# An encoder of mixers and feed-forward layers on one core: the even mixer with the k projection folded into q, gate rows in column groups, and another order of its loop

## The reference

```python
def even_mixer(x, w_in, w_out, ...):
    u_m, z_m, u_r, g_r = _split(x @ w_in, EVEN_SIZES)
    y_m = mlstm_mixer(u_m, z_m, ...)
    y_r = rglru_mixer(u_r, g_r, ...)
    return jnp.concatenate([y_m, y_r], axis=-1) @ w_out

def mlstm_mixer(u, z, ...):
    c = jax.nn.silu(dw_conv(u, conv_w, conv_b))
    q = blockdiag(c, wq)                       # blocks of 4 x 4
    k = blockdiag(c, wk) / math.sqrt(ML_DH)
    v = blockdiag(u, wv)
    i_pre = einsum(qkv, w_ig) + b_ig           # two directions, four heads
    log_f = log_sigmoid(einsum(qkv, w_fg) + b_fg)
    ...
    return jax.nn.sigmoid(z) * head_norm(h_f + h_b, norm_g, ML_HEADS, True)

def rglru_direction(x, w_a, b_a, w_x, b_x, lam):
    r = jax.nn.sigmoid(blocks(x, w_a) + b_a)
    i = jax.nn.sigmoid(blocks(x, w_x) + b_x)
    a = jnp.exp(-LRU_C * r * jax.nn.softplus(-lam))
    b = jnp.sqrt(1 - a * a) * i * x
    return linear_recurrence(a, b)             # a scan over 256 positions
```

## Time and profile before

| | |
|---|---|
| median of 3 runs | 2524.05 us (2523.3 to 2526.69) |
| span of the profiled execution | 2525.1 us, one core |
| TensorE busy | 2462.0 us, 98% |
| VectorE, ScalarE, GpSimd busy | 1339.9, 902.7, 1054.3 us |
| read from HBM | 216.02 MB |
| even stage | about 394 to 793 us of the span |

### The profile page before, as it was taken

One profiled execution on the slowest core, in us unless ns is written; L12 is line 12 of the kernel. 1 busy time (PEld: TensorE's weight loads), 2 busy tenths in 40 slices (PEclk: granted clock), 3 DMA queues, 4 the chain that ended last, 5 costly groups with the idle time before them and its releaser, 6 DMA issues.

```text
span 2525.1 us, 35148 instructions
## 1 busy us (share of the span) xinstructions
PE 2462.0 (98%) x13062; PEld 2014.1 (80%) x13062; DVE 1339.9 (53%) x1547; ACT 902.7 (36%) x1171; POOL 1054.3 (42%) x484
## 2 busy tenths in 40 slices
PE   8999999998998999999999999999999999999998
PEld 7888886776777888888888888777777887888887
DVE  3333447997777333245333245687887457433335
ACT  3222226786344222214222214455544333322212
POOL 5444443332225444445444445333333334444443
PEclk9999999998999999999999999999999999999999
DMA  5233322221112332322232332222222222233322
GB/s 167 92 100 98 103 79 69 73 63 45 61 53 79 96 99 96 109 92 75 96 100 92 108 110 75 82 79 76 76 77 75 67 84 81 78 99 97 107 92 79
DMA packets 63780, 219.55 MB, mean 87 GB/s; under 512 B 10920, under 2 KB 15016, under 8 KB 63552
## 3 DMA queue, kind: packets, MB, share of 16 engines
q1 hardware_dynamic: 63120, 216.03, 26.5%
q0 software_dynamic: 560, 2.11, 0.2%
HBM read 216.02 MB, written 2.10 MB: 86 GB/s over the span
## 4 chain that ended last, share of the span: by engine, by line
PE 84%; DVE 8%; ACT 4%; issue 2%; POOL 1%; DMA 0%; ACTq 0%; DVEq 0%; POOLq 0%; SPq 0%
PE ps L506 24%; PE ps L508 24%; PE ps L507 24%; PE ps L537 2%; DVE sb_th L1803 1%; PE ps L962 1%; DVE sb_Up L1961 1%; PE ps L663 1%; PE ps L662 1%; PE ps L488 1%; PE ps L661 1%; PE ps L489 1%; PE ps L494 1%; PE ps L667 1%; DVE sb_x L1699 1%
## 5 line engine op out<-in xcount | busy, mean ns | idle before, releaser
L415 POOL TENSOR_TENSOR sb_wl<-sb_raw,sb_wh 128x1024 fp32r<-128x1024 f32 (+1 forms) x376 | 980.9, 2609 | 1399.7 <-ACT sb_wh L1136 1399.6
L1136 ACT ACTIVATE sb_wh<-sb_raw 128x1024 fp32r<-128x1024 f32 (+1 forms) x376 | 419.1, 1115 | 1287.4 <-PE ps L508 1220.7
L506 PE MATMUL ps<-sb_xh,sb_wh 128*128 128x512 f32 x2096 | 831.1, 397 | 1.0 <-DVE sb_rq L2047 0.5
L508 PE MATMUL ps<-sb_xl,sb_wh 128*128 128x512 f32 x2096 | 816.5, 390 | 0.0
L507 PE MATMUL ps<-sb_xh,sb_wl 128*128 128x512 f32 x2096 | 816.1, 389 | 0.0
L506 PEld LDWEIGHTS ps<-sb_xh,sb_wh 128*128 128x128 f32 x2096 | 393.4, 188 | 87.8 <-issue 5.3
L507 PEld LDWEIGHTS ps<-sb_xh,sb_wl 128*128 128x128 f32 x2096 | 393.7, 188 | 82.3 <-issue 3.1
L508 PEld LDWEIGHTS ps<-sb_xl,sb_wh 128*128 128x128 f32 x2096 | 393.4, 188 | 82.4
L1611 DVE SCALAR_TENSOR_TENSOR sb_hf<-sb_sg,ps 128x512 f32<-128x512 f32 x88 | 60.5, 688 | 590.5 <-PE ps L508 565.3
L506 PE MATMUL ps<-sb_hh,sb_wh 128*128 128x512 f32 x616 | 239.7, 389 | 0.8 <-POOL sb_wl L415 0.8
L508 PE MATMUL ps<-sb_hl,sb_wh 128*128 128x512 f32 x616 | 239.7, 389 | 0.0
(11 more groups left out here) (336 smaller groups left out, 2912.5 us busy)
## 6 DMA issues: line engine op xcount, KB each, us to landing
sb_raw<-w_in SPq DMA_DIRECT2D x176, 512.0 KB, 3.5
sb_raw<-w_out SPq DMA_DIRECT2D x64, 704.0 KB, 4.0
sb_raw<-w_od SPq DMA_DIRECT2D x80, 512.0 KB, 3.5
sb_raw<-w_ev SPq DMA_DIRECT2D x40, 512.0 KB, 3.5
sb_raw<-w_evo SPq DMA_DIRECT2D x8, 512.0 KB, 3.5
sb_raw<-w_odo SPq DMA_DIRECT2D x8, 512.0 KB, 3.5
sb_x<-x_in SPq DMA_DIRECT2D x8, 256.0 KB, 5.7
out<-sb_x SPq DMA_DIRECT2D x16, 128.0 KB, 1.8
```

The lines of the kernel that those rows point to most:

```text
L415: pool.tensor_tensor(wl[:, sl.par, 0:n], raw[:, sl.par, 0:n], wh[:, sl.par, 0:n].bitcast(F32), ALU.subtract).then_inc(lo_done, 1)
L506: pe.matmul(out, w_h, rh(k), start=start and k == 0, stop=False)
L508: mm = pe.matmul(out, w_h, rl(k), start=False, stop=stop and k == kt - 1)
L1136: act.activation(wh[:, sl.par, 0:kt * P], raw[:, sl.par, 0:kt * P], ACT.Copy).then_inc(hi_done, 1)
```

## The change

- **k is folded into q.** A constant, wkr, holds the blocks of wk; VectorE multiplies it with wq's at the start, and q' = c (wq wk^T) then meets c itself in the scores. The tile k_all holds c, the silu's output, and no k is computed or copied.
- **Gate rows.** The weights sb_gw are 32 columns wide. `inner` adds to four groups of 32 PSUM partitions by 256 columns, one for each part (c or u) and sequence. After the loop two products with a constant, gsel, sort the rows, and all gate arithmetic runs on 100 partitions (ROWS) by 256.
- **Order in the loop.** `inner(t - 1)` stands on TensorE behind slot m of pass t and ahead of `lru_gates(t)`. On VectorE, lru_conv(t + 1) and the weights of pass t + 1 (sb_bd, two of three, double-buffered, and sb_gw) stand behind scans(t) and ahead of recurrent_out(t). On ScalarE the copy to sb_lum and the split of slot u + 2 stand between decay and decay_root, and the copies of q and v ahead of the gate tanhs of the next pass.
- **Heads.** negM and thr are broadcast from four row quadrants, in pairs by sequence (`neg_max`, `margin`); the epsilon is taken out of head_norm (`head_eps`) and stands between the two maxima of the next head; slots z and f are dealt anew (EV_SEQ, EV_GAP1, EV_GAP2), and the product for the values uses other PSUM banks and stands behind the first neg_max of the next head.
- **Constants.** Ten DMAs in place of eight.

```diff
 for t, name in ((vec, "vec"), ..., (gb, "gb"), (sel, "sel"),
+                (wkr, "wkr"), (gsel, "gsel")):
     pool.dma_start(t[:], a[name]).then_inc(const_in, 16)
...
 # TensorE, inner(t)
-pe.matmul(ps[:, bq, :], bd[:, 0, :], cc[:], ...).then_inc(q_mm, 1)
-pe.matmul(ps[:, bk, :], bd[:, 1, :], cc[:], ...).then_inc(k_mm, 1)
-pe.matmul(ps[:, 6, :], gw[:, 0, :], cc[:], start=t == 0, stop=False)
-pe.matmul(ps[:, 6, :], gw[:, 1, :], u, start=False, stop=t == KD - 1)
+pe.wait_ge(lu_ev, min(t + 2, KD))
+pe.matmul(ps[:, Q_BANK, :], bd[:, t % 2, 0, :], k_all[:, t, :], ...).then_inc(q_mm, 1)
+for s_ in range(2):
+    for q in range(SEQS):
+        y = CW * (2 * s_ + q)
+        mm = pe.matmul(ps[y:y + CW, 6, 0:L], gw[:, t % 2, s_, :],
+                       um[:, q, 2:2 + L] if s_ else k_all[:, t, part(q)], ...)
...
 # TensorE, the loop
+for t in range(1, KD):
+    pe.wait_ge(u_ev, t)
+    of_x(0, sl(ev_m(t)))
+    inner(t - 1)
+    lru_gates(t)
+    if t < KD - 1:
+        pe.wait_ge(q_ev, t)
+        of_x(1, sl(ev_u(t + 1)))
+    pe.wait_ge(vt_ev, t)
+    of_x(2, sl(ev_g(t)))
...
 # VectorE, the loop
-if t < KD - 1:
-    lru_conv(t + 1)
 scaled_input(t)
 scans(t)
-if t < KD - 1:
-    recurrent_out(t)
+if 1 <= t < KD - 1:
+    lru_conv(t + 1)
+    weights(t + 1)
+recurrent_out(t)
...
 # VectorE, the heads
     dve.tensor_tensor(rec[:, d, :], rec[:, d, :], ps[:, 4 + d, :], ALU.max).then_inc(dmax_done, 1)
+    if d == 0 and h >= 1:
+        head_eps(h - 1, 7, rs[:])
...
 # order of the sixteen slots of the heads
+EV_SEQ = ("z00", "z01", "f0", "f1", "f2", "f3", "z10", "z11", "f4", "f5", "z20", "z21", "f6", "z30", "z31", "f7")
+EV_GAP1 = ((26,), (29,), (32, 33), (36,))
+EV_GAP2 = ((27, 28), (30, 31), (34, 35), (37, 38))
```

More of the change, by code:

```diff
@@ L799, in early_out, with neg_max @@
[L799 to L808, removed]
+                def neg_max(h, q):
+                    pe.wait_ge(mb_mm, 4 * h + 2 * q)
+                    for d in range(2):
+                        y = CW * (2 * d + q)
+                        pe.matmul(ps[:, 2 + d, part(q)], sel[y:y + NH, h, :], negM[y:y + NH, :], start=True,
+                                  stop=True).then_inc(mb_mm, 1)
@@ new lines, in margin, with values @@
+                def margin(h, q):
+                    pe.wait_ge(marg_mm, 4 * h + 2 * q)
+                    for d in range(2):
+                        y = CW * (2 * d + q)
+                        pe.matmul(ps[:, 4 + d, part(q)], sel[y:y + NH, h, :], thr[y:y + NH, :], start=True,
+                                  stop=True).then_inc(marg_mm, 1)
+                def values(h):
+                    pe.wait_ge(att_done, h + 1)
+                    for z in range(HT):
+                        for q in range(SEQS):
+                            for sb_ in range(SB):
+                                o = (HT * h + z) * P
+                                mm = pe.matmul(ps[:, 4 + z, q * L:(q + 1) * L], vT[:, q * SB + sb_, o:o + P],
+                                               att[:, q, sb_, :], start=sb_ == 0, stop=sb_ == SB - 1)
+                    mm.then_inc(pv_mm, 1)
@@ L829, in even @@
+                        neg_max(h, 0)
+                        values(h - 1)
+                        neg_max(h, 1)
+                        if h >= 2:
+                            pe.wait_ge(hvar_in, h - 1)
+                        keys_queries(h)
+                    for n in EV_GAP1[h]:
+                        head_slot(n)
+                    if h == 0:
                         pe.wait_ge(thr_done, 1)
                         pe.wait_ge(gT_ev, 1)
-                        for d in range(2):
-                            margin(d)
@@ new lines, in even @@
+                split(KD, sl(4))
+                silu(0)
+                lru_in(1)
+                split(KD, sl(5))
+                gelu(0)
+                gates(0)
+                decay(0)
+                decay_root(0)
+                for t in range(1, KD):
+                    last = t == KD - 1
+                    split(KD, sl(ev_m(t) + 2))
+                    query_out(t - 1)
+                    inner_in(t)
+                    value_out(t - 1)
+                    gates(t)
+                    silu(t)
+                    decay(t)
+                    if not last:
+                        lru_in(t + 1)
@@ L1332, in even @@
                         split(KD, sl(ev_u(t + 1) + 2))
[L1333 removed]
                     decay_root(t)
[L1335 to L1341 removed]
+                    split(KD, sl(ev_g(t) + 2))
+                    gelu(t)
                 ln_and_exp()
+                act.wait_ge(rows_mm, 1)
@@ L1381, in even @@
                         act.activation(E[:], E[:], ACT.Exp).then_inc(e_done, 1)
-                    if h >= 1:
-                        act.wait_ge(att_done, h)
+                    for n in EV_GAP1[h]:
+                        split(KD, sl(n + 2))
                     for d in range(2):
```

462 lines of the change are left out of this document (208 added, 254 removed).

## The result

| | before | with the change |
|---|---|---|
| median | 2525.37 us (4 runs, 2523.3 to 2526.87) | 2556.87 us (4 runs, 2555.78 to 2559.12) |
| ratio | | 1.0127, 95% interval 1.0115 to 1.0139 |
| span of the profiled execution | 2525.1 us | 2554.0 us |

The change makes the kernel 31.5 us slower. One execution each of two later experiments (e9 and e11) was disturbed and is left out of their ratios; the trace of e11 is of that one, and no row of it is read.

The account below looks back on a forecast made before the run. It took a closed loop over ScalarE and VectorE (12.7 + 11.9 = 24.6 us a pass) as the bound, not TensorE. Its terms, +20.4 + 2.4 - 0.6 - 5.1 + 3.1 + 3.6 - 3.5 + 1.1, sum to +21.4: 2545 us, range 2528 to 2558.

Parts of the forecast that it names:

- The closed loop: Passes 1 to 6, ScalarE and VectorE: lru_conv and weights enter the loop, period 24.6 to 28.0 us, +20.4 in all.
- the rival of a third meeting: A third GpSimd subtraction slips behind the root and delays VectorE: 12.6 us more, 2558; chance 0.08.
- Lower clock of TensorE: Gates after TensorE's wait for sb_lx run at 1.2 GHz, delaying the fourth tanh by some 0.4: +2.4 over six passes.
- Passes 0 and 1: -0.6: Gates of pass 0 behind one slot and the gelu, +1.6; a 2.2 stretch in pass 1 goes; together -0.6 us.
- From the last gates to the first head: -5.1: Gate arithmetic on 100 partitions by 256: first early output slot ends at 40.0 us where it was 45.1.
- Heads: +3.1 and +3.6: Fourteen pairs at 0.63 us replace three visits of 1.91: +3.1; head_eps holds up att_done, 1.2 in heads 1 to 3: +3.6.
- Tail: -3.5: Hole of 3.2 ahead of the last head_var and 2.1 of lower clock go; 1.1 and 0.7 come back.
- Column groups: TensorE's gate rows, four products of 32 columns by 256: 0.63 us instead of 1.72, 1.1 us saved a pass.
- Start: +1.1: Two more DMAs on GpSimd's queue, 0.53 us each, ahead of a subtraction TensorE already waits for: +1.1 us.
- The rival that TensorE is the bound: TensorE's 98% busy sets the time, so its savings and the closed holes count: about 2499 us; chance 0.05.
- the loop without any meeting: Rival: both subtractions fall into ScalarE's part, pass 23.8 us, six passes give -4.8: about 2516; chance 0.08.

Follow-up runs that it names:

- e9: e6 plus a GpSimd wait for mix_done(t - 1) before the subtraction for slot g(t) in passes 1 to 6: 2517.1 us, ratio 0.996.
- e11: The kernel before with only the GpSimd wait for mix_done before the subtraction for slot g(t): 2522.7 us, ratio 0.9991.
- e8: The changed kernel with four more, useless products on TensorE ahead of lru_gates in each of passes 2 to 7: 2552.8 us.
- e1: The changed kernel with lru_conv(t + 1) and the weights put back ahead of scaled_input(t) on VectorE: 2542.8 us, ratio 1.0067.
- e6: The changed kernel with the edits of e1 and e2, and the copy to sb_lum and split of slot u + 2 ahead of decay: 2518.8 us.
- e2: The changed kernel with ScalarE's split of slot 5 moved behind decay(0): 2551.0 us.
- e5: The changed kernel with SyncE's load of slot u(t + 1) ahead of that of lbd(t) and its wait for TensorE's gates: 2548.4 us.
- e10: e9 plus SyncE's order, slot u(t + 1) loaded ahead of lbd(t): 2516.1 us, ratio 0.9967.
- e12: e10 plus recurrent_out(7) behind the gate arithmetic on VectorE, as in the kernel before: 2511.0 us, ratio 0.9949.
- the best version: The changed kernel with six edits of order alone (e1, e2, e5, e6, e9, e12): 2511.0 us, ratio 0.9949 to the kernel before.

## Why the prediction was right, and where its sum was off

The forecast was 2545 us, slower with 0.78, in a range of 2528 to 2558. Measured: 2556.9, slower, inside the range. The sum was +21.4 us and the measured difference is +31.5; of the 10.1 that are missing, one term holds 8.1, and two others, both mainly by the lower clock, hold 2.1 and 2.2; heads, tail and start together came out 2.4 under their terms.

- **The closed loop.** Shown. A period of 28.0 us was forecast; e8, which takes the lower clock away, has 27.9. VectorE meets two subtractions a pass, where the prediction put them: one right behind the root (on L1802), one at the start of lru_conv. The third stands ahead of the root, as forecast; it ends 0.1 us behind it (507.97 for 507.87), just as VectorE begins, so the rival of a third meeting was near but didn't come true in this pass. e1 and e6 took the loop down again, and the time followed.
- **Lower clock of TensorE.** Mis-sized: 0.4 us a pass, measured 0.9 (28.8 less the 27.9 of e8), so that passes 2 to 6 came to +21.1 for a forecast of 5 x 3.8 = 19.0. The gates take 4.7 and 5.8 in turn, and it is the third tanh that waits longest for them.
- **Passes 0 and 1: -0.6.** Here the prediction failed. With 3.8 for pass 1 from the other two terms it had +3.2 for the two passes; measured were +11.3, and the 8.1 between them is the wait that e2 took away (7.8). The step followed the gates of pass 0 behind one slot and the gelu on TensorE, and did not follow the moved gates into SyncE's queue, where the load of sb_lbd waits for them and the load of slot 5 stands behind it, for which ScalarE waits ahead of the same gates' tanhs. "Each queue that a step is moved past" has to include those that wait for it. e2 and e5 show it from two sides. That the sum came out near is no credit to this term.
- **From the last gates to the first head: -5.1**, measured -2.9. The sign holds and the 7.0 us hole is gone; but z01 ends 5.5 us ahead of sb_gi, as forecast, and the scores behind that wait take 5.4 us in place of 5.3: it is sb_gi that came 1.7 later than counted (29.6 us behind the last tanhs' start, for 27.9). That is the lower clock once more: the last tanhs wait for the gates, and the root comes 13.0 us behind their start, for 11.2 counted. The wait of 5.5 is 2.1 in e10, and e12, which moves recurrent_out(7) out of its way, takes away the rest.
- **Heads: +3.1 and +3.6.** The first is right to the digit: six pairs and eight pairs at 0.63 us. The second didn't happen, and was mis-added too: its own figures, 16.8 against 15.8, give 1.0 a head and not 1.2. head_eps between the two maxima held up TensorE hardly at all: TensorE's wait for sb_att is 0.2 us in all. **Tail: -3.5**: the hole of 3.2 and the lower clock behind it are gone, 5.2 us in all, and 1.6 of wait for sb_wl is new. The remainder is some 2 us more. At least a part of it lies in the instructions next to the visits to the tiled form (values 3.65 for 3.26 to 3.56, the first sum 0.54 for 0.43), which no term had; the rest isn't traced. In all, heads and tail were forecast at +3.2 and measured +1.8.
- **Column groups.** Forecast 0.63 us for the four products, measured 0.57. By the Trainium skill ("TensorE: Matmul & The Clock Gate", section "Measured speedup vs the span model") I had put an estimate of 0.72 beside it, from three groups. The four here run in a third of the 1.72 us that four in a row would take.
- **Start: +1.1**, measured +0.1. TensorE's wait for GpSimd's subtraction is there (0.9 and 0.3 us, as before) and didn't grow by the two DMAs.

The rival that TensorE is the bound falls with e8: more work on TensorE, and a shorter kernel. No run has the loop without any meeting; e9 took one of two out of the way of the scans, at 0.7 to 1.0 us a pass.

## What to carry to other kernels

Two engines that wait for each other once a pass are a bound, whatever share the third one shows: add up the closed chain and compare it with the period, and put each operation where its engine would otherwise wait and nobody waits for it. When a step is moved later, look up who waits for it in the DMA queues, and what stands behind that wait; here one load queued so cost 8 us in one pass. And savings on an engine that isn't the bound bring nothing until that bound is lower: the 2 us a pass saved on TensorE are worth some 0.7 a pass even in the best version, by an estimate from its pitch of 23.5 and TensorE's own 24.2 us of before. The larger part of its 13.7 us comes from behind the loop.

## What the runs showed of the hardware

- Products of 32 output columns in four column groups run side by side in fp32: two groups start 10 ns apart, and four products of 256 columns take 0.57 us with the change of form.
- Behind a wait of 3.8 us on TensorE the gates took 4.7 and 5.8 us for 3.04, with a granted clock of 0.65 and 0.54. With work of no use in the gap they took 3.14 at 1.00, and the kernel was 4 us faster.
- A GpSimd subtraction that meets VectorE's chain cost it 2.0 to 2.1 us in each of these cases, whatever the operation (3.30 for 1.22, 2.62 for 0.55, 2.66 for 0.49, 4.35 for 2.33). So the length of a pass depends on where they meet: behind the root the pass paid for it, and at the convolution 1.05 us of it was waited for.
